# Two transformer blocks on one core: preparations woven into the first product of a stage, head changes in two parts, modulation groups moved

## What is computed

```python
# first block, layer i of 2; ml, mc: six shift/scale/gain rows each, silu(c) @ w_mod[i] + b_mod[i]
hl = rmsnorm(xl, g_pre_mix[i]) * (1 + ml[1]) + ml[0]          # hc alike for the context
zl = hl @ w_in[i]                                            # queries, keys' latent, convolutions
k, v = keys_values(zc), keys_values(zl)                      # 256 context keys, then 512 latent ones
o = softmax(q @ k.T) @ v                                     # 8 heads of 96 and 64
y = concat(rmsnorm(o), rmsnorm(conformer), rmsnorm(shortconv)) @ w_o[i]
xl = xl + ml[2] * rmsnorm(y, g_post_mix[i])
h2 = rmsnorm(xl, g_pre_mlp[i]) * (1 + ml[4]) + ml[3]
xl = xl + ml[5] * rmsnorm(relu(h2 @ w_mlp_in[i])**2 @ w_mlp_out[i], g_post_mlp[i])
# the context does the same in layer 0; in layer 1 only its keys and values are needed
# second block, layer i of 2
qa, ka, va, za, ba, aa, ub, zb, qc, kc, vc, zc, iq, ik, iw, gates = split(rms_norm(x) @ w_in_2[i])
ya = gated_delta_rule(silu(conv4(qa)), silu(conv4(ka)), silu(conv4(va)), beta, decay)
x = x + (sum over branches of sigmoid(gates) * (branch @ w_branch_2)) @ w_out_2[i]
```

## Time and profile before

| | us |
|---|---|
| runs before | 3335.54, 3342.18 (median), 3342.20 |
| the profiled execution | 3340.34, its span 3339.0 |
| PE busy | 2981.5 |
| POOL busy | 1679.1 |
| DVE busy | 1534.1 |
| ACT busy | 1039.9 |

### The profile page before, as it was taken

The page is one execution under the profiler, slowest core; times in us unless marked ns, Lnnn a source line. Parts: engine busy times, 40 slices in busy tenths (PEclk is TensorE's granted clock), DMA queues, the critical chain, the costliest instruction groups (busy, mean ns, idle before and its releaser), DMA issues.

```text
span 3339.0 us, 41499 instructions
## 1 busy us (share of the span) xinstructions
PE 2981.5 (89%) x16384; PEld 2429.2 (73%) x16384; DVE 1534.1 (46%) x2534; ACT 1039.9 (31%) x1702; POOL 1679.1 (50%) x1240
## 2 busy tenths in 40 slices
PE   6787888897999968888999989999889899998988
PEld 5566567786888756566888777888767778886766
DVE  3548454324122348453122256544682275437742
ACT  3232344333222332343222243222322333222331
POOL 4364225886555654234555555445525554446344
PEclk8778999998999989898999989999999999999998
DMA  7234222453333221222333222111212221112122
GB/s 286 70 102 145 84 99 71 144 176 101 95 95 95 84 90 60 76 73 68 95 95 95 86 67 82 58 52 53 77 53 70 74 90 59 58 53 68 58 69 70
DMA packets 81217, 291.71 MB, mean 87 GB/s; under 512 B 9088, under 2 KB 9344, under 8 KB 80640
## 3 DMA queue, kind: packets, MB, share of 16 engines
q1 hardware_dynamic: 81024, 289.06, 26.8%
HBM read 286.93 MB, written 2.10 MB: 87 GB/s over the span
## 4 chain that ended last, share of the span: by engine, by line
PE 69%; DVE 15%; POOL 7%; ACT 4%; issue 4%; DMA 1%; SPq 0%; ACTq 0%; POOLq 0%; DVEq 0%
PE ps L568 50%; PE ps L541 5%; DVE t L2008 3%; PE ps L688 3%; POOL t L2561 2%; DVE t L2339 2%; PE ps L708 2%; PE ps L928 1%; PE ps L937 1%; PE ps L860 1%; PE ps L596 1%; PE ps L942 1%; POOL t L2581 1%; POOL t L2754 1%; DVE t L2432 1%
## 5 line engine op out<-in xcount | busy, mean ns | idle before, releaser
L568 PE MATMUL ps<-t,t 128*128 128x512 f32 (+3 forms) x9936 | 2262.7, 387 | 127.7 <-POOL t L2561 45.6
L568 PEld LDWEIGHTS ps<-t,t 128*128 128x128 f32 x9936 | 1817.2, 193 | 499.8 <-issue 97.9
L2561 POOL TENSOR_TENSOR t<-t,t 128x1024 fp32r<-128x1024 f32 (+3 forms) x444 | 1052.4, 2376 | 700.8 <-ACT t L1214 685.2
L1214 ACT ACTIVATE t<-t 128x1024 fp32r<-128x1024 f32 (+3 forms) x444 | 458.3, 1035 | 1061.8 <-PE ps L568 996.9
L541 PE MATMUL ps<-t,t 128*128 128x128 f32 (+2 forms) x1540 | 248.2, 301 | 159.8 <-DVE t L1797 66.7
L541 PEld LDWEIGHTS ps<-t,t 128*128 128x128 f32 (+2 forms) x1540 | 187.7, 150 | 229.3 <-DVE t L1797 49.5
L2092 DVE TENSOR_TENSOR t<-t 128x512 f32<-128x512 f32 (+1 forms) x96 | 65.8, 685 | 340.6 <-ACT t L1463 340.6
L2008 DVE SCALAR_TENSOR_TENSOR t<-t,t,t 128x512 f32<-128x512 f32 (+1 forms) x180 | 157.3, 874 | 6.4
L2754 POOL TENSOR_TENSOR t<-t,t 128x512 fp32r<-128x512 f32 (+1 forms) x96 | 127.1, 1324 | 58.6 <-DVE t L1773 54.6
L2104 DVE TENSOR_TENSOR t<-ps,t 128x512 f32<-128x512 f32 x60 | 40.9, 691 | 216.4 <-PE ps L568 216.4
L2581 POOL TENSOR_TENSOR t<-t,t 128x4 f32<-128x4 f32 (+2 forms) x93 | 88.4, 950 | 86.0 <-DVE t L1805 51.8
(11 more groups left out here) (252 smaller groups left out, 2654.3 us busy)
## 6 DMA issues: line engine op xcount, KB each, us to landing
t<-in_wbig SPq DMA_DIRECT2D x412, 512.0 KB, 3.5
t<-in_wmod SPq DMA_DIRECT2D x96, 512.0 KB, 5.9
t<-in_wbig SPq DMA_DIRECT2D x16, 416.0 KB, 3.1
t<-in_wbig SPq DMA_DIRECT2D x14, 256.0 KB, 2.7
t<-in_wbig SPq DMA_DIRECT2D x8, 332.0 KB, 2.8
t<-in_wbig SPq DMA_DIRECT2D x6, 384.0 KB, 2.9
t<-in_x SPq DMA_DIRECT2D x1, 2048.0 KB, 13.1
out<-t SPq DMA_DIRECT2D x1, 2048.0 KB, 6.6
```

The source lines that it names most:

```text
L568: m = p.matmul(out, lhs, rhs, start=kk == 0 and n == 0, stop=kk == tiles - 1 and n == 2)
L1214: a.activation(c.hi(w), c.raw(w), ACT.Copy).then_inc(w_hi.h, w_hi.up(("cut", w)))
L2561: g.tensor_tensor(c.lo(w), c.raw(w), c.hi(w).bitcast(F32), ALU.subtract).then_inc(w_lo.h, w_lo.up(("cut", w)))
```

## The change

1. *Head changes.* `load_head` turns queries and the first four key tiles, and waits only for the copy of those; `load_rest` turns the last two key tiles two steps later, in l0 and l1.
2. *Modulation groups 6 to 11 of layer 0* are woven into the heads of c0 at rate 0.4; they stood in c0's projection and l0's mixing.
3. *One more step of the heads* is taken before c0's, l0's and l1's projection.
4. *Preparations of c0, l0, mc0, l1, ml1, d0, d1*: the last four or five steps are woven at rate 0.5 into the first product, on every engine that takes part. The residuals of c0 and l0 follow these steps on DVE and POOL.
5. *c1 and l1*: l1's sums of squares and norm factors are written between the parts of c1.
6. *Residual of the perceptrons*: DVE multiplies by the row while the sums go on (`gained`), and the last loop is one instruction a tile.
7. *Second block*: `qa` is the first product, `sm` the second; the small product `gc` follows `ka`, and DVE's four-tap convolutions of qa begin after `sm` and the decays.

```diff
-IN2 = {"sm": [(2048, 2056), (5128, 5452)], "qa": [(0, 512)], "ka": [(512, 1024)], "va": [(1024, 1536)],
+IN2 = {"qa": [(0, 512)], "sm": [(2048, 2056), (5128, 5452)], "ka": [(512, 1024)], "va": [(1024, 1536)],
...
+def then(steps, work, *args):
+
+    yield from steps
+    work(*args)
...
         def load_head(h):
-            b = h % 2
-            k0s = list(range(0, nk, 4))
-            Q = pair(heads, ("head", n, h), (act, ("qt", n, h)), (dve, ("kt", n, h)))
+            Q = pair(heads, ("head", n, h), (act, ("qt", n, h)), (dve, ("ktr", n, h, 0)))
+            kept.add(c.where[("head", n, h)])
...
+        def load_rest(h):
+            done(("head", n, h))
+            if h >= 2 and nk <= 4:
+                return
+            Q = c.pair(("head", n, h))
+            opened(c.where[("head", n, h)], ((dve, ("kt", n, h)),))
+            for k0 in k0s[1:]:
+                turns([Q[0:64, 128 * j:128 * j + 128] for j in range(nk - k0)],
+                      [c.KTM[:, k0 + j, 64 * h:64 * h + 64] for j in range(nk - k0)], ("kt", n, h, k0))
...
+            if u % nt == 2 and u // nt + 1 < NH:
+                load_rest(u // nt + 1)
...
-        yield from prep(f"d{i}")
+        first = onward(prep(f"d{i}"), 5)
         ready = prepared(f"d{i}")
+        yield from weave(delta_in(i, ("qa",)), first, 0.5)
         yield from product_gemm(("sm", i), "TM", (c.AH, c.AL), 512, 332, 8, ready, lambda b: ((act, ("sm", i, b)),))
-        yield from delta_in(i)
+        yield from delta_in(i, ("ka", "va", "za"))
...
-    run(g)
-    run(weave(mix("c0"), mods(0, 4, 6, main), 0.06))
-    rest = onward(heads("c0"), 2 * NH + 2)
+    onward(g, 3)
+    run(weave(weave(mix("c0"), mods(0, 4, 6, main), 0.06), g, 0.5))
+    rest = onward(weave(heads("c0"), mods(0, 6, 12, [6, 7]), 0.4), 2 * NH + 2)
     row_of("c0", 0, 0, 1)
+    next(rest)
     g = prep("l0")
-    more = mods(0, 6, 12, main)
-    run(weave(weave(project("c0"), both(rest, g, 4), 0.5), more, 0.09, finish=False))
-    run(g)
-    run(weave(mix("l0"), more, 0.09))
+    run(weave(project("c0"), both(rest, g, 4), 0.4))
+    next(g)
+    run(weave(mix("l0"), g, 0.5))
...
-    run(mix("c1"))
-    run(prep("l1"))
-    run(mix("l1"))
+    keys = onward(mix("c1"), 9)
+    g = onward(prep("l1"), 4)
+    next(keys)
+    next(g)
+    run(keys)
+    run(weave(mix("l1"), g, 0.5))
...
-            if row is None:
-                v.scalar_tensor_tensor(x[:, t, :], y[:, t, :], r[:, t:t + 1], x[:, t, :], ALU.mult,
-                                       ALU.add).then_inc(dve.h, dve.up(("x", n, t)))
-            else:
-                v.scalar_tensor_tensor(y[:, t, :], y[:, t, :], r[:, t:t + 1], row, ALU.mult, ALU.mult).then_inc(
-                    dve.h, dve.up(("yr", n, t)))
-                V.wait_ge(dve, ("yr", n, t))
-                v.tensor_tensor(x[:, t, :], x[:, t, :], y[:, t, :], ALU.add).then_inc(dve.h, dve.up(("x", n, t)))
+            v.scalar_tensor_tensor(x[:, t, :], y[:, t, :], r[:, t:t + 1], x[:, t, :], ALU.mult, ALU.add).then_inc(
+                dve.h, dve.up(("x", n, t)))
+
+    def gained(n, h, t):
+
+        y = c.Y[n][:, t, 512 * h:512 * h + 512]
+        V.wait_ge(act, ("row", n))
+        V.wait_ge(act, ("ysq", n, h, t))
+        v.tensor_tensor(y, y, c.ROW[n][:, 512 * h:512 * h + 512], ALU.mult).then_inc(dve.h, dve.up(("yg", n, h, t)))
...
+        yield from weave(product_gemm(("ka", i), 4, 8, lambda b: None), convs("qa"), 1.0)
         V.wait_ge(product, ("gc", i))
...
-    run(g)
-    residual("l0")
-    run(mlp("mc0", prep("ml0"), 0.8))
+    next(g)
+    run(weave(mlp("mc0", prep("ml0"), 0.8), then(g, residual, "l0"), 0.5))
```

More of the change, by code:

```diff
@@ L1832, in residual @@
         if row is not None:
-            V.wait_ge(act, ("row", n))
+            for t in range(nt - 1):
+                gained(n, 1, t)
         V.wait_ge(act, ("ysq", n, 1, nt - 1))
@@ L2104, in take, with gains @@
                 v.tensor_tensor(y, B, y, ALU.add).then_inc(dve.h, dve.up(("y", n, g, h, b)))
+        def gains():
+            for t in range(nt):
+                gained(n, 0, t)
+                yield
         def down(g):
-            for h in range(2):
-                yield from product_gemm(("w2", n, g, h), nt, 8, lambda b: take(g, h, b))
+            yield from product_gemm(("w2", n, g, 0), nt, 8, lambda b: take(g, 0, b))
+            yield from weave(product_gemm(("w2", n, g, 1), nt, 8, lambda b: take(g, 1, b)),
+                             gains() if g == 3 else iter(()), 0.5)
         for g in range(4):
@@ L2508, in dve_program @@
     run(mods(0, 0, 4))
-    run(g)
-    run(weave(mix("c0"), mods(0, 4, 6), 0.06))
-    rest = onward(heads("c0"), 2 * NH + 2)
+    onward(g, 3)
+    run(weave(weave(mix("c0"), mods(0, 4, 6), 0.06), g, 0.5))
+    rest = onward(weave(heads("c0"), mods(0, 6, 12), 0.4), 2 * NH + 2)
+    next(rest)
     g = prep("l0")
-    more = mods(0, 6, 12)
-    run(weave(weave(project("c0"), both(rest, g, 4), 0.5), more, 0.09, finish=False))
-    run(g)
-    residual("c0")
+    run(weave(project("c0"), both(rest, g, 4), 0.4))
+    next(g)
+    run(weave(mix("l0"), then(g, residual, "c0"), 0.5))
     V.wait_ge(inputs, 48)
@@ L2529, in dve_program @@
     residual("ml0")
-    run(mix("c1"))
-    run(prep("l1"))
-    run(mix("l1"))
+    keys = onward(mix("c1"), 9)
+    g = onward(prep("l1"), 4)
+    next(keys)
+    next(g)
+    run(keys)
+    run(weave(mix("l1"), g, 0.5))
     rest = onward(weave(heads("l1"), mods(1, 6, 12), 0.22), 4 * NH + 2)
+    next(rest)
     run(weave(project("l1"), rest, 0.4))
     residual("l1")
-    run(prep("ml1"))
-    run(mlp("ml1", iter(()), 0.0))
+    g = onward(prep("ml1"), 5)
+    run(weave(mlp("ml1", iter(()), 0.0), g, 0.5))
     residual("ml1")
@@ L2867, in delta_in @@
     def delta_in(i):
-        for k in range(4):
-            g.memset(c.U4[:, k, 0:3], 0.0).then_inc(pool.h, pool.up(("pad4", i)))
         def convs(key):
@@ L2939, in layer @@
     def layer(i):
-        yield from prep(f"d{i}")
+        first = onward(prep(f"d{i}"), 5)
+        yield from weave(product_gemm(("qa", i), 4, 8, lambda b: None), first, 0.5)
+        G.wait_ge(pool, ("pl", f"d{i}", 7))
+        for k in range(4):
+            g.memset(c.U4[:, k, 0:3], 0.0).then_inc(pool.h, pool.up(("pad4", i)))
         yield from product_gemm(("sm", i), 4, 8, lambda b: None)
@@ L2960, in pool_program @@
     run(mods(0, 0, 4))
-    run(steps)
-    run(weave(mix("c0"), mods(0, 4, 6), 0.06))
-    rest = onward(heads("c0"), 2 * NH + 2)
+    onward(steps, 3)
+    run(weave(weave(mix("c0"), mods(0, 4, 6), 0.06), steps, 0.5))
+    rest = onward(weave(heads("c0"), mods(0, 6, 12), 0.4), 2 * NH + 2)
+    next(rest)
     steps = prep("l0")
-    more = mods(0, 6, 12)
-    run(weave(weave(project("c0"), both(rest, steps, 4), 0.5), more, 0.09, finish=False))
-    run(steps)
-    residual("c0")
-    run(weave(mix("l0"), more, 0.09))
+    run(weave(project("c0"), both(rest, steps, 4), 0.4))
+    next(steps)
+    run(weave(mix("l0"), then(steps, residual, "c0"), 0.5))
     rest = onward(weave(heads("l0"), mods(1, 0, 6), 0.22), 4 * NH + 2)
+    next(rest)
     steps = prep("mc0")
     run(weave(project("l0"), both(rest, steps, 4), 0.4))
-    run(steps)
-    residual("l0")
-    run(mlp("mc0", prep("ml0"), 0.8))
+    next(steps)
+    run(weave(mlp("mc0", prep("ml0"), 0.8), then(steps, residual, "l0"), 0.5))
     residual("mc0")
@@ L2978, in pool_program @@
     residual("ml0")
-    run(mix("c1"))
-    run(prep("l1"))
-    run(mix("l1"))
+    keys = onward(mix("c1"), 9)
+    steps = onward(prep("l1"), 4)
+    next(keys)
+    next(steps)
+    run(keys)
+    run(weave(mix("l1"), steps, 0.5))
     rest = onward(weave(heads("l1"), mods(1, 6, 12), 0.22), 4 * NH + 2)
+    next(rest)
     run(weave(project("l1"), rest, 0.4))
     residual("l1")
-    run(prep("ml1"))
-    run(mlp("ml1", iter(()), 0.0))
+    steps = onward(prep("ml1"), 5)
+    run(weave(mlp("ml1", iter(()), 0.0), steps, 0.5))
     residual("ml1")
```

134 lines of the change are left out of this document (84 added, 50 removed).

## The result

The change is slightly slower. Its median is 3349.10 us over 8 runs (3346.52 to 3353.99), beside 3341.91 for the kernel before (8 runs, 3334.65 to 3344.58); the ratio is 1.0029 with a 95% interval of 1.0019 to 1.0038. The forecast was 3331 us and a gain of 10.8. The profiled execution has a span of 3348.5 us where it had 3339.0.

What follows compares the result with a forecast made beforehand. PE was busy 89% of the span, so gains could come only from its 357.5 us idle or its clock. The terms summed to -10.8 from 3340.34, 3329.5, stated as 3331 us for compared runs; range 3314 to 3352.

Steps and rivals of the forecast that it cites:

- (d): Preparations woven into the first product at seven places: slower by 14.7 us in sum, bounds +5 and +35.
- rival 5: In mc0, l0's residual and POOL's cuts 60 to 63 take turns: 2 to 6 us, 3336 us; chance 0.05.
- Rival 1: At woven products PE, POOL and ACT wait for each other: some 3 us more a place, 3352 us; chance 0.19.
- (b): Groups 6 to 11 moved from c0's projection and l0's mixing into c0's heads: -3 us, bounds -10 and +5.
- (c): One more head step before the projections of c0, l0 and l1: -3 us, bounds 0 and -6.
- (a): Head switches of l0 and l1, last two key tiles turned two steps later: -16 us, bounds 0 and -22.
- rival 3: Head switches of l0 and l1 only move their wait: the 16 us become 3, 3344 us; chance 0.13.
- (e): `qa` ahead of `sm` in d0 and d1: next product 4.1 us later, +8.2 us for both, bounds 0 and +10.
- Rival 4: In d0 and d1 the order of `qa` and `sm` costs nothing: 3323 us; chance 0.08.
- (f): From c1 to l1, l1's squares start earlier and the keys' products fill the wait: -8.7 us, bounds -14 and -2.
- (g): ml1's residual shortened by multiplying the row in during the sums: -3 us, bounds -2 and -4.
- Rival 2: PE's clock rises in c0's heads or elsewhere, perhaps 9 us gained on the path: 3322 us; chance 0.13.

Runs made afterwards that it cites:

- run 5: The changed kernel with each of the seven woven preparations taken one step further before its first product; 3310.46 us, 0.9909 of the kernel before.
- run 1: The changed kernel with all seven preparations ahead of their first product again, the rest kept; 3326.49 us, 0.9962 of the kernel before.
- run 3: The changed kernel with modulation groups 6 to 11 back in c0's projection and l0's mixing; 3353.62 us, 1.0043 of the kernel before.
- run 9: The kernel of run 4 with groups 6 to 11 moved into c0's heads and c0's extra head step; 3316.65 us, 0.9938 of the kernel before.
- run 4: The kernel before with only split head switches, l1's sums between c1's parts and rows multiplied in during the sums; 3312.99 us, 0.9927 of the kernel before.
- Run 11: The kernel of run 4 with only ml1, d0 and d1 woven, one step further ahead, and `qa` first; 3311.84 us, 0.9913 of the kernel before.
- run 10: The kernel of run 4 with one more head step before the projections of c0, l0 and l1; 3319.67 us, 0.9930 of the kernel before.
- run 2: The changed kernel with the preparations of mc0 and ml1 ahead of the first product again; 3336.31 us, 0.9996 of the kernel before.

## Why the prediction was wrong

**(d) The weave, the step that failed.** The step was "the nearest thing in the trace is ml0's preparation in mc0's product ... one unit takes 6.84 us, or some 7.3". The row was read rightly, but in it no matmul waits for the columns. In the change PE waits for the column, the column stands behind a cut, and the cut waits for PE's last unit: 7.9 us at full clock and 9.4 at a lower one (run 5 opens the circle and shows 6.8). Term (d) of +14.7 measured +22 (run 1). The excess lies in two places: ml1's +1 was +6.5, and mc0's +3.5 was +8.7. ml1 is this circle, with the lower clock on top. In mc0 the product's own end and the earlier squares came out at +3.9, near the forecast; the other 4.8 came with the residual beside the four cuts, which is rival 5 (2 to 6 us) and not the circle. l0's and d's places came out as put: the circle turned there too, but its 7.86 us in d0 is only half a us a unit over the 7.3 put. What the prediction left out altogether is that one more step ahead opens it.

**Rival 1** had the sign, the mutual wait and nearly the time (3352, measured 3349.1): PE, ACT and POOL each waiting for another, with the clock lower on top. That the time fits is in part luck. Its "units of columns from 7.3 to about 8" came from 24 matmuls at 7.5 us for 5.7, that is from the low clock; measured were 7.9 with the matmuls at 5.78, and 9.4 with the lower clock. Its "3 us more a place" was 5.5 in ml1, under 1 in c0 and nothing in d0 and d1, and c0's heads, l1's projection and the two stretches of heads, which it doesn't touch, make 14.7 us of the error. I gave it 0.19 and spoke against it with "there the second product's tail shared the queues"; what I had to ask was which engine's end POOL's cut waits for, and what stands behind that cut. Of my signs of being wrong, c0's heads longer by 20 us came true; PE's waits inside ml1's product were 0.4 to 2.2 us each, not over 4.

**(b) The groups**, forecast -3: removed as forecast, while the heads of c0 grew by 20.2, not 13.4. "Fetch and steps are about level" was the failing step: in c0's heads PE waited 12.8 us in 3 for the groups' DMAs, up to 5.9 at once, and the issues held SP's queue for 50 us where I had put 44. Of what left l0's mixing, 8.5 us came back as a new wait in the value products for DVE's copies (L834 <- L2118); the total of that stretch was still as forecast. By runs 3 and 9 the move is worth some 5 us one way or the other.

**(c) The head step**, forecast -3: no gain in any run, and l1's projection was 3 us longer. Its basis, half of an idle time, was no measurement.

**(a) The head switches**, forecast -16: right. Alone they gave -14.7 (run 4), in the change -12.1. Of the waits of 1.70 us for the queries' copy one a layer is left (the total fell from 16.3 us in 17 to 5.4 in 6), so rival 3 falls.

**(e) `qa` ahead of `sm`**, forecast +8.2: right in the traces. With nothing woven (run 1) d0's start and d1 are 3.4 and 3.7 us longer than before. Rival 4 falls.

**(f)** -8.7 measured -8.8; even unwoven (run 4) 5.4 us of the 15.8 gained at the first column are given back by the end of `cf`. **(g)** -3 measured -3.5.

**Rival 2**, the clock, came in part: the mean granted clock rose from 0.941 to 0.950. In c0's heads, where the rival had put it, it rose from 0.63 to 0.77, and the stretch still became 20 us longer. Windows of the kernel after (length, PE, PEld, DVE, ACT and POOL busy, clock, DMA share, GB/s):

```profile
135.00:210.00 75.00, 49.94 (x606) 36.29 (x605) 21.56 (x85) 23.52 (x77) 20.66 (x29) 0.77 0.48 169
```

The rest of d0 gained 6.8 us that no term had, and 5.3 of them fall into one place near its end. Windows of that place, kernel before and then, with the same matmuls in them, after:

```profile
2560.00:2580.00 20.00, 17.20 (x61) 12.78 (x59) 11.33 (x17) 3.18 (x3) 11.09 (x7) 0.83 0.27 79
2580.00:2600.00 20.00, 17.16 (x63) 13.41 (x62) 5.60 (x8) 2.12 (x2) 10.98 (x7) 0.83 0.18 52
```

```profile
2570.00:2590.00 20.00, 15.55 (x63) 11.06 (x62) 13.95 (x20) 3.19 (x3) 12.43 (x8) 1.00 0.25 79
2590.00:2605.00 15.00, 13.80 (x61) 11.42 (x62) 2.81 (x5) 2.12 (x2) 9.67 (x5) 1.00 0.23 71
```

The same 124 matmuls take 40 us before and 35 after, with PE busy 34.4 and 29.4, and no edit touches this place. Run 11 has the drop although its d stages are woven, run 5 has not. What decides it is not shown. In the profiled execution it hid a part of the loss: without it the span would have been some 5 us longer still.

## What to carry to other kernels

Before a step is woven into a product, write down for one round which engine's end each instruction waits for. Where that list comes back to its start, the round's length is the sum of the circle, not the busiest engine's share, and moving the side work one step ahead opens it (here 39 us for one step, some 5 of them from a residual that moved along with it). A period read from a place where nobody waits for the result doesn't price a place where somebody does. And where several small parts are made at once, measure them apart: this change held 26 us of gain under a weave that was one step out of phase.

## What the runs showed of the hardware that was not expected

The clock in c0's heads differs widely between kernels whose work there is the same, in one profile of each: 0.59, 0.50 and 0.74 below. Windows from about the first to the last of its steps, in the kernel before, in run 10 and in run 4 (the last is 49 us long, since the same steps were done sooner):

```profile
129.00:184.00 55.00, 42.61 (x220) 32.44 (x219) 20.78 (x79) 21.91 (x71) 20.31 (x27) 0.59 0.00 1
```

```profile
130.00:185.00 55.00, 45.63 (x212) 34.03 (x211) 20.41 (x77) 22.16 (x71) 19.61 (x25) 0.50 0.00 1
```

```profile
126.00:175.00 49.00, 36.51 (x217) 27.25 (x216) 20.37 (x79) 22.20 (x71) 19.81 (x26) 0.74 0.00 1
```

0.50 means that the clock stood on its lower level (1.2 GHz) all the time, 0.74 that it was on the higher one (2.4 GHz) about half of it. That is 6 us of one stretch. In a profile a difference of 5 to 7 us in a stretch of small steps with many waits is therefore no evidence for an edit by itself: several kernels' traces or the runs in rounds have to agree. ml1's +6.5 has run 2 behind it; the +20.2 of c0's heads is against a kernel before at 0.59 and carries this uncertainty.
